# Gated delta stage: 16x16 substitution split in two, two panel splits moved, group loop written out

## The chip, the cores and the metric

The kernel runs on one core of one Trainium2 chip, in one launch. The metric is the device time in microseconds (us), the median of several executions. The profile is taken from one further execution.

## The reference, cut to what matters

The program computes a first transformer block and then a second one, for 512 tokens plus 16 meta tokens (528 in all), width 1024, in float32. The second block begins with a gated delta layer, and only that layer is touched here. Per head it solves, in each chunk of tokens, a unit lower triangular system and then runs a recurrence over the chunks:

```python
m = jnp.einsum('bhnid,bhnjd->bhnij', kb, k) * jnp.where(strict, decay, 0.0)
eye = jnp.eye(C, dtype=jnp.float32)
rhs = jnp.concatenate([vb, kb * jnp.exp(gc)[..., None]], axis=-1)
sol = lax.linalg.triangular_solve(m + eye, rhs, left_side=True, lower=True, unit_diagonal=True)
```

Before that, the projections of the normalised input pass through a causal convolution over four tokens and a SiLU, and the query and key heads are normalised to length 1.

## The kernel before, in words

**Tiling.** Features lie on the 128 partitions, tokens along the free axis. The 16 value heads are worked on in four groups (`NG` = 4, `gdn_group(g, first)`), four heads each. The chunks are one of 16 meta tokens (c = 0) and four of 128 tokens; `ORDER` is (1, 2, 3, 4, 0).

**Groups.** TensorE, VectorE, ScalarE and GpSimd run group 0 written out and groups 1 to 3 in a hardware loop (`mla_loop`, with `Fori`, so that waits are made on counts held in registers). The sync engine's queue is written out for all four groups already.

**Weights.** They come as a stream of panels of 512 KB through a ring of four slots (`raw`). For each panel the sync engine issues the load (`refill`, line 561), ScalarE makes the high part (`split_high`, line 291) and GpSimd the low part (`split_low`, line 296); `low(j)` in GpSimd's group is the split of the group's panel j + 2, since the splits run two panels ahead. `weights(j)` on the sync engine refills the slot of panel j, and waits until panel j has its low part, that is for `low(j - 2)`. Every product is three matmuls of high and low parts (`mm3`, lines 301 to 303).

**First part of a group.** TensorE makes eight projections `project(0..7)` into two pairs of PSUM banks in turn, 48 matmuls each. VectorE applies the convolution (`taps(t)`: line 1351 and three times line 1358), a clamp (line 510) between ScalarE's exponentials, and the product `gated(t)` (line 1368). A projection waits until the convolution has read its banks: `project(7)` waits for `taps(5)`, `project(8)` for `taps(6)`. `l2_scale` (line 1374) normalises query and key heads. Two more projections, `project(8)` and `project(9)`, belong to the output gate.

**The triangular system.** `first_m(c)` (line 1395) makes the matrix of a chunk on VectorE. The sync engine writes each of the four big chunks' matrices to DRAM (`m_out`, line 575) and reads their 16x16 diagonal blocks back, one block per partition (line 585, into `lane_w`). The queue's order is

```python
for j in range(7):
    weights(j)
m_out(1)
m_out(2)
weights(7)
m_out(3)
m_out(4)
```

and then the wait for all four, the read at line 585, `weights(8)` and `weights(9)`. On VectorE `substitute()` waits for the read (`LANES_IN`), sets the diagonal (line 1432), and inverts all blocks at once by forward substitution: for each k from 1 to 14 a product (line 1438) and a subtraction (line 1442), and at the end a transposed copy (line 1444). The sync engine, which waits for that copy, writes both results to DRAM (lines 590, 591) and reads them back by rows (line 594, into `row_w` and `row_wt`).

GpSimd then masks them into the matrices `TN` (line 644, four times), VectorE into `U` (`turned_16`, line 1450, four times). From there 15 steps (`STEPS`) join blocks of 16 to blocks of 128: in each, GpSimd masks a matrix (line 655, buffer `CL`), TensorE multiplies twice (lines 2161 and 2126) and transposes, ScalarE and VectorE copy and subtract. Steps 4, 9 and 14 are those of the short chunk of 16 tokens. The first step needs the first mask of line 655. After the steps comes the recurrence over the chunks, with parts of the gate's projections and of the output projection of the group before put between.

**Order around the change.** GpSimd issues `low(0)` to `low(7)`, the mask of the short chunk (line 637, needs `first_m(0)`), `low(8)`, `low(9)`, then waits for the rows. VectorE issues `gated(6)`, `substitute()`, `taps(7)`, `first_m(0)`, `attend(0)` (line 1409), `gated(7)`. TensorE waits for `attend(0)` (`g_at`) and for ScalarE's decays (`g_eabs`) ahead of `project(9)`.

Of the kernel before, what the change touches and what calls it, by code (L numbers as in the profile page):

```python
# [21 lines left out]
NG = 4  # L22
HG = 4
QUERY_TILES = (0, 2, 1, 3)
CHUNKS = 5
# [10 lines left out]
P_GDN = P_FF + 64  # L36
# [17 lines left out]
BLK = 16  # L54
# [33 lines left out]
def build(nc, A, out):  # L88
    ctx = ExitStack()
    with ctx:  # L90
# [173 lines left out]
        def sem(name):  # L264
            if name not in sems:
                sems[name] = ctx.enter_context(nc.semaphore(name))
            return sems[name]
# [220 lines left out]
        def gdn_panel(j, g):  # L488

            return (P_GDN + j, None, 0) if isinstance(g, int) and g == 0 else (P_GDN - 4 + j, g, 16)  # L490

# [9 lines left out]
        def mla_loop(engine, group):  # L501

            group(0, True)
            with engine.Fori(1, NG) as g:
                group(g, False)
# [26 lines left out]
        def gst(i, n, k):  # L532

            return i * n + k
# [5 lines left out]
        def _(sp):  # L540
# [26 lines left out]
            def gdn_group(g, first):  # L567
# [29 lines left out]
                for j in range(10, 12 if first else 16):  # L597
                    weights(j)
            for g in range(NG):
                gdn_group(g, g == 0)  # L600
            rest = STREAM - RING - (P_KV - RING)
# [12 lines left out]
        def _(pool):  # L614
# [13 lines left out]
            def gdn_group(g, first):  # L628
                def low(j):
                    p, i, length = gdn_panel(j, g)  # L630
                    split_low(pool, p + AHEAD, i, length)

                for j in range(8):
                    low(j)

                pool.wait_ge(sem("g_m1"), gst(g, CHUNKS, CHUNKS))
                pool.tensor_tensor(C0[0][0:META, :, 0:META], M[0][0:META, :, 0:META], level_mask(0, META),
                                   ALU.mult).then_inc(sem("g_c0"), 1)
                low(8)
                low(9)  # L640
                pool.wait_ge(sem("lanes_moved"), gst(g, ROWS_IN, ROWS_IN))
                pool.wait_ge(sem("l2_done"), gst(g, 4, 4))
                for c in ORDER[:LATER]:
                    pool.tensor_tensor(by_block(TN[c]), spread(row_w, c), block_mask(NEG_TRIL_16), ALU.mult)\  # L644
                        .then_inc(sem("g_t16"), 1)
                for s, (l, c) in enumerate(STEPS):
                    n = tokens(c)[1]
                    if s == 0 and not first:

                        pool.wait_ge(sem("z_lo"), gst(g, 4, 0))  # L650
                    if s == 1:
                        pool.wait_ge(sem("g_t16"), gst(g, LATER, LATER))
                    if s >= 2:
                        pool.wait_ge(sem("g_q"), gst(g, NS, s - 1))
                    pool.tensor_tensor(CL[s % 2][0:n, :, 0:n], M[c][0:n, :, 0:n], level_mask(l, n),  # L655
                                       ALU.mult).then_inc(sem("g_cl"), 1)
                for j in range(10, 12 if first else 16):
                    low(j)
            mla_loop(pool, gdn_group)
            for t in range(5):  # L660
# [16 lines left out]
        def _(act):  # L677
# [185 lines left out]
            def gdn_group(g, first):  # L863
# [161 lines left out]
                for t in range(4):  # L1025
                    high_y(t)
            mla_loop(act, gdn_group)
            def square_out(k):
# [122 lines left out]
        def _(dve):  # L1151
# [184 lines left out]
            def gdn_group(g, first):  # L1336
# [88 lines left out]

                def substitute():

                    w, wt = lane(lane_w), lane(lane_wt)
                    dve.wait_ge(sem("lanes_moved"), gst(g, ROWS_IN, LANES_IN))
                    if not first:  # L1430
                        dve.wait_ge(sem("z_lo"), gst(g, 4, 0))
                    dve.memset(lane_w[:, 0:BLK * BLK:BLK + 1], -1.0).then_inc(sem("g_lane"), 1)
                    for k in range(1, BLK - 1):
                        n = BLK - 1 - k
# [7 lines left out]
                        dve.tensor_tensor(below, below, tmp, ALU.subtract).then_inc(sem("g_lane"), 1)  # L1442
                    dve.wait_ge(sem("g_lane"), gst(g, LANE_OPS, LANE_OPS - 1))
                    dve.tensor_copy(wt, w.rearrange("p i j -> p j i")).then_inc(sem("g_lane"), 1)

# [30 lines left out]
                conv_clamp(4)  # L1476
                gated(4)
                taps(5)
                conv_clamp(5)
                l2_scale(2)  # L1480
                l2_scale(3)
                gated(5)
                taps(6)
                conv_clamp(6)
                gated(6)
                substitute()
                taps(7)
# [144 lines left out]
                low_y(3)  # L1632
            mla_loop(dve, gdn_group)
            for m in range(8):
# [174 lines left out]
        def _(pe):  # L1809
# [177 lines left out]
            def gdn_group(g, first):  # L1987
# [105 lines left out]
                project(8, 0)  # L2093
                pe.wait_ge(sem("g_at"), gst(g, CHUNKS, 1))
                pe.wait_ge(sem("g_eabs"), gst(g, CHUNKS * HG, CHUNKS * HG))
                pe.wait_ge(sem("l2_ln"), gst(g, 4, 4))
# [47 lines left out]
                for s, (l, c) in enumerate(STEPS):  # L2144
# [20 lines left out]
                    if s:  # L2165
                        join(s - 1)
                    if s == 1:
                        level_0()
                    if s - 2 in TURNED:
# [119 lines left out]
                out_tile(7)  # L2289
            mla_loop(pe, gdn_group)  # L2290
            pe.wait_ge(sem("g_vb"), CHUNKS * NG)
# [308 lines left out]
```

## Time and profile before

| | |
|---|---|
| median of 3 runs | 2154.03 us (2152.55 to 2160.12) |
| the profiled execution | 2150.23 us |
| its span, first to last instruction | 2148.4 us |
| mean granted TensorE clock | 0.951 of full speed |
| VectorE's substitution in the second group | 1044.68 to 1053.8 us |
| the same in the first group | 867.78 to 876.9 us |

PE is TensorE, DVE VectorE, ACT ScalarE, POOL GpSimd, SP the sync engine (SPq: its queue of DMA issues). Times in a timeline are microseconds from the start of the span; a row gives the start, the duration, engine, line, operation, output and inputs, and in brackets the idle time of the engine before it with what ended it. A row with x2, x3 and so on merges several instructions. The gated delta stage goes from about 808 to 1565 us, and its four groups begin near 808, 985, 1179 and 1374 us.

### The profile page before, as it was taken

How to read it: one execution, taken by the hardware profiler on the slowest of the kernel's cores; microseconds unless marked ns; L12 is line 12 of the kernel's file. 1: busy time of each engine (PE TensorE's matmuls, PEld its weight loads, DVE VectorE, ACT ScalarE, POOL GpSimd, SP SyncE). 2: the span in 40 equal slices, each digit the busy share in tenths (PEclk: the TensorE clock that was granted, in tenths of full speed). 3: DMA queues.
4: the chain of work that ended last, by engine and by line, in shares of the span. 5: the costliest groups of instructions: out<-in, count | busy, mean ns of one | idle time of the engine just before them, and what ended most of it. 6: DMA issues, size and time to landing. Idle time of an engine off the chain costs nothing.

```text
span 2148.4 us, 30354 instructions
## 1 busy us (share of the span) xinstructions
PE 1951.1 (91%) x11197; PEld 1620.1 (75%) x11269; DVE 1018.5 (47%) x1765; ACT 821.6 (38%) x1477; POOL 684.8 (32%) x334
## 2 busy tenths in 40 slices
PE   6999999799999979699699969988978999999994
PEld 4677777578778759688699969978967776777773
DVE  6422232613132255656746655575555455454544
ACT  4555632432232335226324523451335333333322
POOL 3132244343443422411431242125134212222212
PEclk9999999999999989889889989998989999999997
DMA  5112123132322303201301221131031111211111
GB/s 178 50 61 67 59 88 98 41 107 80 106 92 80 104 29 102 70 21 31 101 21 41 80 52 40 42 92 40 30 100 55 62 31 52 61 55 47 60 49 39
DMA packets 72898, 140.23 MB, mean 65 GB/s; under 512 B 30544, under 2 KB 40016, under 8 KB 72656
## 3 DMA queue, kind: packets, MB, share of 16 engines
q1 hardware_dynamic: 72064, 134.33, 20.2%
q10 hardware_dynamic: 720, 4.33, 0.5%
q8 instruction: 78, 1.28, 0.2%
q14 instruction: 36, 0.29, 0.0%
HBM read 129.13 MB, written 9.50 MB: 65 GB/s over the span
## 4 chain that ended last, share of the span: by engine, by line
PE 31%; issue 19%; POOL 8%; DVE 4%; ACT 2%; POOLq 0%; ACTq 0%; DVEq 0%
PE ps L301 6%; PE ps L302 6%; PE ps L303 6%; POOL wsp L296 5%; PE ps L2456 3%; PE ps L2425 2%; PE ps L2424 2%; POOL ov L644 1%; PE ps L2446 1%; PE ps L2161 1%; PE ps L2126 1%; POOL aux_f L655 1%; POOL work L655 1%; DVE aux_f L1358 1%; PE ps L2428 0%
## 5 line engine op out<-in xcount | busy, mean ns | idle before, releaser
L296 POOL TENSOR_TENSOR wsp<-raw,wsp 128x1024 fp32r<-128x1024 f32 x231 | 558.1, 2421 | 1282.1 <-ACT wsp L291 1282.1
L301 PE MATMUL ps<-h_split,wsp 128*128 128x264 f32 (+1 forms) x1488 | 524.5, 352 | 59.9 <-DVE ov L1409 41.0
L302 PE MATMUL ps<-h_split,wsp 128*128 128x264 f32 (+1 forms) x1488 | 511.5, 344 | 0.0
L303 PE MATMUL ps<-h_split,wsp 128*128 128x264 f32 (+1 forms) x1488 | 510.9, 343 | 0.0
L301 PEld LDWEIGHTS ps<-h_split,wsp 128*128 128x128 f32 x1488 | 289.3, 194 | 99.7 <-issue 56.2
L302 PEld LDWEIGHTS ps<-h_split,wsp 128*128 128x128 f32 x1488 | 288.9, 194 | 31.6
L303 PEld LDWEIGHTS ps<-h_split,wsp 128*128 128x128 f32 x1488 | 288.0, 194 | 32.4
L291 ACT ACTIVATE wsp<-raw 128x1024 fp32r<-128x1024 f32 x231 | 240.7, 1049 | 105.0 <-PE ps L303 103.7
L301 PE MATMUL ps<-y_split,wsp 128*128 128x512 f32 (+1 forms) x496 | 195.3, 394 | 12.9 <-DVE y_split L463 5.8
L302 PE MATMUL ps<-y_split,wsp 128*128 128x512 f32 (+1 forms) x496 | 191.7, 386 | 0.0
L303 PE MATMUL ps<-y_split,wsp 128*128 128x512 f32 (+1 forms) x496 | 191.0, 385 | 0.0
L301 PEld LDWEIGHTS ps<-y_split,wsp 128*128 128x128 f32 x496 | 94.8, 191 | 34.6 <-issue 14.6
L303 PEld LDWEIGHTS ps<-y_split,wsp 128*128 128x128 f32 x496 | 94.6, 191 | 19.2
L302 PEld LDWEIGHTS ps<-y_split,wsp 128*128 128x128 f32 x496 | 94.6, 191 | 18.6
L1293 DVE TENSOR_TENSOR work<-work,ps 128x512 f32<-128x512 f32 x32 | 22.0, 687 | 151.8 <-PE ps L303 151.8
L1761 DVE TENSOR_REDUCE tiny<-ps 128x1 f32<-128x144 f32 (+1 forms) x64 | 32.4, 506 | 112.6 <-PE ps L2428 112.6
L301 PE MATMUL ps<-y_late,wsp 128*128 128x264 f32 x256 | 75.8, 296 | 7.5 <-DVE work L1564 3.2
L1285 DVE TENSOR_TENSOR work<-work 128x512 f32<-128x512 f32 x32 | 29.4, 920 | 107.9 <-ACT work L819 107.9
L2456 PE MATMUL ps<-ov 128*128 128x128 f32 (+1 forms) x448 | 80.5, 307 | 0.0
L963 ACT ACTIVATE qs_f<-ps 128x512 f32<-128x512 f32 (+2 forms) x60 | 27.7, 462 | 133.3 <-PE ps L2161 133.3
L1358 DVE SCALAR_TENSOR_TENSOR aux_f<-ps,cwg,aux_f 128x528 f32<-128x528 f32 x96 | 73.8, 769 | 3.4
L2456 PEld LDWEIGHTS ps<-ov 128*128 128x128 f32 (+1 forms) x448 | 60.5, 192 | 18.5 <-issue 10.2
(346 smaller groups left out, 3237.1 us busy)
## 6 DMA issues: line engine op xcount, KB each, us to landing
raw<-in_w SPq DMA_DIRECT2D x231, 512.0 KB, 3.5
m_home<-ov SPq DMA_DIRECT2D x16, 256.0 KB, 4.4
x_home<-x_res ACTq DMA_DIRECT2D x1, 2112.0 KB, 6.7
x_res<-x_home ACTq DMA_DIRECT2D x4, 528.0 KB, 6.7
x_res<-in_x SPq DMA_DIRECT2D x4, 512.0 KB, 5.3
out<-x_res SPq DMA_DIRECT2D x8, 256.0 KB, 2.0
mats<-in_mats SPq DMA_DIRECT2D x1, 640.0 KB, 7.3
rope<-in_rope SPq DMA_DIRECT2D x1, 528.0 KB, 5.1
```

The source lines that it names most:

```text
L291: act.activation(wsp[:, s, 0, :], raw[:, s, :], ACT.Copy).then_inc(hi_ready, 1)
L296: pool.tensor_tensor(wsp[:, s, 1, :], raw[:, s, :], wsp[:, s, 0, :].bitcast(F32), ALU.subtract).then_inc(lo_ready, 1)
L301: pe.matmul(o, wh, xh, start=start, stop=False)
L302: pe.matmul(o, wh, xl, start=False, stop=False)
L303: return pe.matmul(o, wl, xh, start=False, stop=stop)
L655: pool.tensor_tensor(CL[s % 2][0:n, :, 0:n], M[c][0:n, :, 0:n], level_mask(l, n), ALU.mult).then_inc(sem("g_cl"), 1)
L1285: dve.tensor_tensor(relu2[b], relu[b], relu[b], ALU.mult).then_inc(sem("ff_sq"), 1)
L1358: dve.scalar_tensor_tensor(out=shifted, in0=x, scalar=cwg[:, 4 * t + k:4 * t + k + 1], in1=shifted, op0=ALU.mult, op1=ALU.add)\
L1761: dve.tensor_reduce(tiny[:, 4 + b:5 + b], s_ap, AX.X if i < 3 else AX.XY, ALU.max)\
L2424: pe.matmul(PS[:, bank_, 0:w], qn, KN[:, h, lo_:hi_], start=True, stop=False)
L2425: last = pe.matmul(PS[:, bank_, 0:w], qr, krope[r, lo_:hi_], start=False, stop=True)
L2456: last = pe.matmul(o_bank(b), VT[0:n, c, h * P:(h + 1) * P], PT[b][0:n, c, :], start=c == 0, stop=c == i + 1)
```

## The change: what it does

- VectorE: `substitute(k0, k1)` now does the rows k0 to k1 - 1. `substitute(1, 7)` stands between `gated(4)` and `taps(5)` and holds the wait for the blocks; `substitute(7, 15)` with the transposed copy stands between the clamp of tile 6 and `gated(6)`. `taps(6)` is moved ahead of `gated(5)`.
- GpSimd: `low(8)` and `low(9)` are taken from the place ahead of the row masks and put before the masks of steps 5 and 10 (`CHUNKS` is 5).
- TensorE: the waits for `attend(0)` and the decays are moved from ahead of `project(9)` to step 1 of the joining, ahead of `level_0()`.
- TensorE, VectorE, ScalarE and GpSimd: all four groups are written out (`gdn_groups`), with waits on constants.

```diff
--- before.py
+++ after.py
@@ -487,7 +487,12 @@
 
         def gdn_panel(j, g):
 
-            return (P_GDN + j, None, 0) if isinstance(g, int) and g == 0 else (P_GDN - 4 + j, g, 16)
+            return P_GDN + (16 * g - 4 if g else 0) + j, None, 0
+
+        def gdn_groups(group):
+
+            for g in range(NG):
+                group(g, g == 0)
 
         def mla_panel(j, g):
 
@@ -596,8 +601,7 @@
                       .then_inc(sem("lanes_moved"), 16)
                 for j in range(10, 12 if first else 16):
                     weights(j)
-            for g in range(NG):
-                gdn_group(g, g == 0)
+            gdn_groups(gdn_group)
             rest = STREAM - RING - (P_KV - RING)
             with sp.Fori(0, rest // RING) as i:
                 for s in range(RING):
@@ -636,8 +640,6 @@
                 pool.wait_ge(sem("g_m1"), gst(g, CHUNKS, CHUNKS))
                 pool.tensor_tensor(C0[0][0:META, :, 0:META], M[0][0:META, :, 0:META], level_mask(0, META),
                                    ALU.mult).then_inc(sem("g_c0"), 1)
-                low(8)
-                low(9)
                 pool.wait_ge(sem("lanes_moved"), gst(g, ROWS_IN, ROWS_IN))
                 pool.wait_ge(sem("l2_done"), gst(g, 4, 4))
                 for c in ORDER[:LATER]:
@@ -650,13 +652,15 @@
                         pool.wait_ge(sem("z_lo"), gst(g, 4, 0))
                     if s == 1:
                         pool.wait_ge(sem("g_t16"), gst(g, LATER, LATER))
+                    if s in (CHUNKS, 2 * CHUNKS):
+                        low(7 + s // CHUNKS)
                     if s >= 2:
                         pool.wait_ge(sem("g_q"), gst(g, NS, s - 1))
                     pool.tensor_tensor(CL[s % 2][0:n, :, 0:n], M[c][0:n, :, 0:n], level_mask(l, n),
                                        ALU.mult).then_inc(sem("g_cl"), 1)
                 for j in range(10, 12 if first else 16):
                     low(j)
-            mla_loop(pool, gdn_group)
+            gdn_groups(gdn_group)
             for t in range(5):
                 split_low(pool, P_KV - 4 + AHEAD + t)
             norm_add_odd(pool, "nC", NK, ALL)
@@ -1024,7 +1028,7 @@
                     act.wait_ge(used, turn(p + 1, i, length))
                 for t in range(4):
                     high_y(t)
-            mla_loop(act, gdn_group)
+            gdn_groups(gdn_group)
             def square_out(k):
                 norm_square(act, "nC", lambda m: accT[:, m, :], NK, k, lambda m: (sem("g_add"), 8 * NG + m + 1))
             split_high(act, P_KV - 2)
@@ -1423,14 +1427,15 @@
                     dve.tensor_tensor(TN[0][0:n, :, 0:n], mat_h(IDENT, n), C0[0][0:n, :, 0:n], ALU.subtract)\
                        .then_inc(sem("g_t0"), 1)
 
-                def substitute():
+                def substitute(k0, k1):
 
                     w, wt = lane(lane_w), lane(lane_wt)
-                    dve.wait_ge(sem("lanes_moved"), gst(g, ROWS_IN, LANES_IN))
-                    if not first:
-                        dve.wait_ge(sem("z_lo"), gst(g, 4, 0))
-                    dve.memset(lane_w[:, 0:BLK * BLK:BLK + 1], -1.0).then_inc(sem("g_lane"), 1)
-                    for k in range(1, BLK - 1):
+                    if k0 == 1:
+                        dve.wait_ge(sem("lanes_moved"), gst(g, ROWS_IN, LANES_IN))
+                        if not first:
+                            dve.wait_ge(sem("z_lo"), gst(g, 4, 0))
+                        dve.memset(lane_w[:, 0:BLK * BLK:BLK + 1], -1.0).then_inc(sem("g_lane"), 1)
+                    for k in range(k0, k1):
                         n = BLK - 1 - k
                         tmp = lane_tmp[:, 0:n * k].rearrange("p (i j) -> p i j", j=k)
                         below = w[:, k + 1:BLK, 0:k]
@@ -1440,8 +1445,9 @@
                            .then_inc(sem("g_lane"), 1)
                         dve.wait_ge(sem("g_lane"), gst(g, LANE_OPS, 2 * k))
                         dve.tensor_tensor(below, below, tmp, ALU.subtract).then_inc(sem("g_lane"), 1)
-                    dve.wait_ge(sem("g_lane"), gst(g, LANE_OPS, LANE_OPS - 1))
-                    dve.tensor_copy(wt, w.rearrange("p i j -> p j i")).then_inc(sem("g_lane"), 1)
+                    if k1 == BLK - 1:
+                        dve.wait_ge(sem("g_lane"), gst(g, LANE_OPS, LANE_OPS - 1))
+                        dve.tensor_copy(wt, w.rearrange("p i j -> p j i")).then_inc(sem("g_lane"), 1)
 
                 def turned_16(c):
 
@@ -1475,15 +1481,16 @@
                 taps(4)
                 conv_clamp(4)
                 gated(4)
+                substitute(1, 7)
                 taps(5)
                 conv_clamp(5)
                 l2_scale(2)
                 l2_scale(3)
+                taps(6)
                 gated(5)
-                taps(6)
                 conv_clamp(6)
+                substitute(7, BLK - 1)
                 gated(6)
-                substitute()
                 taps(7)
                 conv_clamp(7)
                 first_m(0)
@@ -1630,7 +1637,7 @@
                 low_y(1)
                 low_y(2)
                 low_y(3)
-            mla_loop(dve, gdn_group)
+            gdn_groups(gdn_group)
             for m in range(8):
                 if m % 2 == 0:
                     dve.wait_ge(used, P_KV - 4 + m // 2 + 1)
@@ -2091,8 +2098,6 @@
                 project(7, 2, 4)
                 pe.wait_ge(sem("g_conv"), gst(g, 8, 7))
                 project(8, 0)
-                pe.wait_ge(sem("g_at"), gst(g, CHUNKS, 1))
-                pe.wait_ge(sem("g_eabs"), gst(g, CHUNKS * HG, CHUNKS * HG))
                 pe.wait_ge(sem("l2_ln"), gst(g, 4, 4))
                 project(9, 6)
                 last_of = {}
@@ -2165,6 +2170,8 @@
                     if s:
                         join(s - 1)
                     if s == 1:
+                        pe.wait_ge(sem("g_at"), gst(g, CHUNKS, 1))
+                        pe.wait_ge(sem("g_eabs"), gst(g, CHUNKS * HG, CHUNKS * HG))
                         level_0()
                     if s - 2 in TURNED:
                         turn_u(s - 2)
@@ -2287,7 +2294,7 @@
                 out_tile(6, 2)
                 norm_o(CHUNKS - 1)
                 out_tile(7)
-            mla_loop(pe, gdn_group)
+            gdn_groups(gdn_group)
             pe.wait_ge(sem("g_vb"), CHUNKS * NG)
             pe.wait_ge(sem("g_oln"), CHUNKS * NG)
             for t in range(4):
```

## Rows read from the trace of the kernel before

**Rows 1.** The page: busy time of the engines (share of the span), instructions.

```profile
PE 1951.1 (91%) x11197; PEld 1620.1 (75%) x11269; DVE 1018.5 (47%) x1765; ACT 821.6 (38%) x1477; POOL 684.8 (32%) x334
```

**Rows 2.** TensorE's waits, second group (985 to 1175 us).

```profile
PE ps L301 <- DVE ov L1409: 10.3, 1, 10.3
PE ps L2161 <- POOL work L655: 5.9, 1, 5.9
```

**Rows 3.** Timeline of the sync engine's queue, second group: start, us, line, transfer.

```profile
1034.10 0.35 SPq L561 DMA_DIRECT2D raw<-in_w  x1
1034.54 0.94 SPq L575 DMA_DIRECT2D m_home<-ov  x2
1039.43 0.36 SPq L585 DMA_DIRECT2D ov<-m_home  x1
1041.06 6.75 SPq L561 DMA_DIRECT2D raw<-in_w  x2
1053.85 0.33 SPq L590 DMA_DIRECT2D w_home<-ov  x1
...
1056.46 0.94 SPq L594 DMA_DIRECT2D work<-w_home  x1
```

**Rows 4.** Time from issue to landing of line 585, over the four groups.

```profile
DMA to landing us min/median/max: 2.9/3.0/3.0
```

**Rows 5.** Time from issue to landing of line 594, over the four groups.

```profile
DMA to landing us min/median/max: 2.9/3.3/3.8
```

**Rows 6.** Timeline of VectorE, second group: start, us, line, operation, [idle before].

```profile
1031.31 0.76 DVE L1351 TENSOR_SCALAR aux_f<-ps,cwg 128x528 f32<-128x528 f32 x1
...
1036.46 0.71 DVE L1374 SCALAR_TENSOR_TENSOR work<-work,ov 128x528 f32<-128x528 f32 x1 [0.22 <-ACT ov L894]
...
1038.30 0.76 DVE L1351 TENSOR_SCALAR aux_f<-ps,cwg 128x528 f32<-128x528 f32 x1
...
1044.68 0.07 DVE L1432 MEMSET ov<- 128x16 f32 x1
...
1045.21 2.26 DVE L1438 TENSOR_TENSOR work<-ov 128x26 f32<-128x26 f32 x1
...
1049.66 0.22 DVE L1438 TENSOR_TENSOR work<-ov 128x56 f32<-128x56 f32 x1
...
1060.82 8.71 DVE L1450 TENSOR_TENSOR aux_f<-work,mats 128x512 f32<-128x512 f32 x4
```

**Rows 7.** Timeline of GpSimd, second group.

```profile
1031.68 2.39 POOL L296 TENSOR_TENSOR wsp<-raw,wsp 128x1024 fp32r<-128x1024 f32 x1 [7.08 <-ACT wsp L291]
1038.67 2.36 POOL L296 TENSOR_TENSOR wsp<-raw,wsp 128x1024 fp32r<-128x1024 f32 x1 [4.60 <-ACT wsp L291]
1045.00 2.43 POOL L296 TENSOR_TENSOR wsp<-raw,wsp 128x1024 fp32r<-128x1024 f32 x1 [3.97 <-ACT wsp L291]
...
1060.43 5.17 POOL L296 TENSOR_TENSOR wsp<-raw,wsp 128x1024 fp32r<-128x1024 f32 x2 [1.43 <-ACT wsp L291]
1065.56 6.29 POOL L644 TENSOR_TENSOR ov<-aux_f,mats 128x512 f32<-128x512 f32 x4
1071.81 1.25 POOL L655 TENSOR_TENSOR work<-ov,mats 128x512 f32<-128x512 f32 x1
...
1083.37 1.28 POOL L655 TENSOR_TENSOR aux_f<-ov,mats 128x512 f32<-128x512 f32 x1 [3.70 <-PE ps L2161]
```

**Rows 8.** Line 644 over all four groups: ns min/median/max.

```profile
L644 POOL TENSOR_TENSOR ov<-aux_f,mats x16: 1248/1702/1749, 888.7 to 1459.6; 128x512 f32<-128x512 f32 x16
```

**Rows 9.** TensorE by stretch: us, busy (instructions), granted clock, DMA.

```profile
1040.00:1048.97 8.97, 8.96 (x75) 1.00 0.40 90
...
1059.26:1063.26 4.00, 4.00 (x18) 0.50 0.06 9
```

**Rows 10.** TensorE's waits where the third group begins (1176 to 1183 us).

```profile
PE ps L301 <- issue: 2.7, 2, 1.7
```

**Rows 11.** TensorE's waits where the fourth group begins (1370 to 1378 us).

```profile
PE ps L301 <- issue: 2.1, 2, 1.4
```

## The prediction

> **What bounds the kernel now.** I read the page first: TensorE is busy 91% of the span [rows 1], so what a change in this stage is worth lies in TensorE's few waits. The view of its waits for the second group shows two that matter: 10.3 us ahead of `project(9)`, put down to line 1409 (`attend(0)`), and 5.9 us ahead of the first joining step, put down to GpSimd's first mask [rows 2]. The first comes from VectorE's order: `attend(0)` is issued behind the whole substitution and `taps(7)`. The second is the end of a chain: copy of the substitution done at 1053.8, write to DRAM issued 1053.85, last read back issued 1056.46 [rows 3], landed within 2.9 to 3.8 us [rows 5], so by 1060.3. Four masks of line 644 start at 1065.56, behind two panel splits that began at 1060.43, and the first step mask starts at 1071.81 [rows 7] and ends at 1073.06. From there the group runs its joining and recurrence, which the change leaves in order. So the question is not whether the 10.3 us go, but when that first step mask ends. All four groups have this shape; I work in the times of the second and multiply by four.
>
> **The change, part by part.**
>
> *Waits moved on TensorE.* `project(9)` no longer waits. Nothing of the 10.3 us is gained by that alone: `project(9)` took some 7.8 us from 1059.26 and ended near 1067, and TensorE then stood 5.9 us. The joining starts with the mask, not with TensorE.
>
> *First half of the substitution.* It needs the blocks on VectorE. The timeline of the queue says when they come: `weights(7)` goes out at 1034.10, the last two `m_out` at 1034.54, the read of the blocks at 1039.43 [rows 3], landing 2.9 to 3.0 us later [rows 4], at 1042.4. `weights(7)` waits for `low(5)`, which ends at 1031.68 + 2.39 = 1034.07 [rows 7]; that split follows ScalarE's work for tile 4, all ahead of the new wait, and the change touches neither it nor the queue's order. VectorE reaches `substitute(1, 7)` after `gated(4)`, at 1031.3, where `taps(5)` starts now [rows 6]. It will stand there for 1042.4 - 1031.3 = 11.1 us. Queued behind it are `taps(5)` and all the rest of VectorE's work; ScalarE's exponentials of tile 5, split 6, and TensorE's `project(7)` wait for that.
>
> Its own work: from the memset at 1044.68 to the product of k = 7 at 1049.66 is 4.98 us, in which one product took 2.26 us where a wider one takes 0.22 [rows 6]. That one ended at 1047.47, as GpSimd's split at 1045.00 + 2.43 did [rows 7]: the operation stood behind the split. Without that it is 4.98 - 2.1 = 2.9 us. GpSimd has nothing to do at 1042.4 to 1045.3, since `low(6)` waits for tile 5. End: 1045.3.
>
> *Tile 5, then tile 6.* From `taps(5)` at 1031.31 to the end of `l2_scale(3)` at 37.17 are 5.8 us [rows 6]: `taps(6)`, now next, starts at 1051.1 and ends 3.2 us later (one operation of 0.76 us [rows 6] and three like it), at 1054.3. Before it started at 1038.30. The move of `taps(6)` ahead of `gated(5)` saves the 1.2 us between these two rows, already counted so. `low(6)` came 7.36 us after the start of `taps(5)` [rows 6, 7]: now 1052.7 to 1055.05. `gated(5)`, two inputs in SBUF, stands behind it until 1055.05 and ends at 1055.6; the clamp ends at 1056.0.
>
> *Second half.* From 1049.66 to 1053.74, where `taps(7)` follows now, is 4.1 us of work [rows 6]. ScalarE's two exponentials and its split put `low(7)` 2.4 us after the clamp, as now (42.6 to 1045.00, [rows 7]): 1058.4 to 1060.8. The substitution stands behind it for 2.4 us again. End: 1056.0 + 4.1 + 2.4 = 1062.5, against 1053.8: 8.7 us late.
>
> The Trainium skill (SBUF — State Buffer, "Who interferes with whom") states that VectorE with two SBUF inputs and a GpSimd operation that reads SBUF exclude each other for the whole instruction. By that rule the two stops count in full, as above, and it speaks against placing the halves between the splits; a view of SBUF that gave both engines room would make the end 1059.5. The product of 2.26 us agrees with the rule.
>
> *Rows back.* From copy end to rows landed are now 1060.3 - 1053.8 = 6.5 us at most, 5.6 at least (landing 2.9). In the new order `weights(9)` is issued at 1060.8, 1.7 us ahead of the writes; in the queue now it is issued at 1047.5, the second of the pair at 1041.06 + 6.75 [rows 3], far ahead. A panel is 512 KB, a write 128 KB. I add 0.5 us: nothing at the low end; 1.6 us at the high end, about half of a panel's landing of the kind that delays the second pair of `m_out` (4.9 us from 1034.54 to 1039.43 against 3.0 for a read alone). Rows landed: 1062.5 + 6.5 + 0.5 = 1069.5.
>
> *Masks.* The two splits are gone from ahead of them, and the rows themselves set the start. Four masks of line 644 cost 1.25 us each alone and 1.70 each beside VectorE's `turned_16` [rows 8]; the four took 6.29 us because only the first ones met it [rows 7]. Now `turned_16` starts at the same time, so three meet it, and the first step mask too: 1.25 + 3 x 1.70 + 1.25 + 0.45 = 8.05 us. First step mask ends at 1077.55, against 1073.06: **4.5 us later in each group, 18 us in four**. Ends: with rows at 1068.1 and masks alone (6.25 us) 1074.4, +1.3; with rows at 1071.1 and a full 8.5 us 1079.6, +6.5.
>
> *Is TensorE later still?* `project(7)` starts when `taps(5)` is done, 1048.5, so TensorE stands some 13 us before it. After such a stand the granted clock is 0.50 for 4 us, 18 matmuls, against 75 in 8.97 us at full clock [rows 9]. First half to 1053.3, small products 1.3, second half 2.9: 1057.7. `taps(7)`, after `gated(6)`, starts at 1063.2 and is not held up. `project(8)` and `project(9)`, 5.8 each: 1069.4. TensorE has 8 us in hand, so this cold start costs nothing; if that cover went, it would cost some 2 us.
>
> *`low(8)` and `low(9)`.* 2.4 us each. At step 5 GpSimd stood 3.70 us before its mask [rows 7]: covered. Step 10 comes behind a short-chunk mask in the same way, with a stand that is some 0.5 us too short for the split; TensorE takes up a mask later than it is made. I cost both at nothing; without any cover they would cost 2.4 us each. Panels 10 and 11, and the later refills behind them (`weights(10)` and on), are wanted only in the recurrence.
>
> *Groups written out.* The passes of the loop that begin the third and fourth group show TensorE standing for 2.7 and 2.1 us with no releaser [rows 10, 11]. The first group, written out already, and the step from it to the second show no such stand. Gain 4.8 us; bounds 0 (if VectorE's copy of the group's scalars takes the place, as it held TensorE 0.8 us in the second group) and 6. The skill (Runtime: NRT & Kernel Launch, "Instruction fetch mechanics") says a taken branch outside the fetched window forces a fetch. The stands at the loop's turn agree.
>
> **Sum.** +18.0 - 4.8 = +13.2 us on the profiled execution's 2150.2 (2148.4 in the span, 1.8 around it): 2163.4. That execution lies 3.8 us under the median of 2154.0; put on the median the forecast is **2167 us**, +0.6%. Bounds of this case alone: 4 x 1.3 - 6 = -1 us, and 4 x 6.5 = +26; I hold +5 to +20 likely, 2159 to 2174.
>
> **Rivals.**
>
> *The wait is there, and the rest absorbs it: no change.* If GpSimd's splits fall between VectorE's operations and the writes don't queue, the copy ends at 1059.5, rows land at 1065.5, masks end at 1072.5 to 1074: about +0.4 per group, +1.6 - 4.8 = -3 us, 2151. Against it: the stop of 2.26 us, and the splits' places follow from the same exponentials.
>
> *The blocks are in time: faster.* If the read's landing did not stop VectorE at 1031.3, the first half would end at 1036.3 (one stop behind `low(5)`), all later steps 9.0 us earlier than in my account, and the first mask near 1068.5, as TensorE's `project(9)` ends by 59: -4.5 per group, -18 - 4.8 = -23 us, 2131. This decides as soon as the blocks land by about 1036.5; a landing at 1039.3 is break-even with the loop's gain. Only the queue's 1039.43 speaks against it, but plainly.
>
> *The late splits or long code cost.* A step mask behind `low(9)`, or fetching of straight code, at 1 to 2 us per group more: 2172. The first group's even run speaks against the code.
>
> **Chances.** Forecast case 0.66; absorbed 0.19; blocks in time 0.08; the last 0.07. A measurement of this kernel tells about 0.5%, 10.8 us, from no change. The forecast case lies above that in three of four of its outcomes, the last rival too: slower 0.55; same 0.34, from the lower part of the forecast case and the absorbed one; faster 0.11. Range 2150 to 2174: it leaves out the fast rival and the upper tail.
>
> **What the new profile would show.** Right: VectorE idle about 11 us before line 1432, released by the DMA of the blocks; TensorE idle about 13 us before `project(7)`, released by line 1358, none before `project(9)`, and about 8 us before the first line 2161; first step mask some 4.5 us later against the start of the group; no `issue` stands where groups begin. Wrong: a read of the blocks issued much before the time that answers to 1039.4, no stand at line 1432, or line 644 starting where it did.

## The result: 0.9% slower

| | before | changed |
|---|---|---|
| median | 2153.61 us (4 runs) | 2174.78 us (2173.19 to 2176.77, 4 runs) |
| profiled execution | 2150.23 us | 2175.55 us |
| span | 2148.4 us | 2173.8 us |
| mean granted clock | 0.951 | 0.943 |

The ratio is 1.0086 with a 95% interval of 1.0070 to 1.0101. The changed kernel is slower by 15 to 22 us by that interval. Forecast were 13 us more and a range up to 2174.

The page of the changed kernel, busy times and the costliest chain by engine:

```profile
PE 1955.4 (90%) x11197; PEld 1621.3 (75%) x11269; DVE 1016.7 (47%) x1765; ACT 821.7 (38%) x1477; POOL 685.0 (32%) x334
...
PE 44%; DVE 9%; ACT 3%; DMA 3%; issue 2%; POOL 2%; SPq 0%; ACTq 0%; POOLq 0%; DVEq 0%
```

TensorE has the same 11197 matmuls as before [rows 1] and is busy 4 us longer with them, at a lower mean clock; the other 21 of the 25 us by which the span grew are idle time. Its waits in the second group, which answer to [rows 2] (the window is shifted, since the group begins later):

```profile
PE ps L301 <- DVE aux_f L1362: 12.9, 1, 12.9
PE ps L2166 <- POOL work L659: 9.1, 1, 9.1
PE ps L2024 <- DVE cwg L1347: 2.8, 1, 2.8
```

The wait for `attend(0)` is gone. In its place stands one for line 1362, the last operation of `taps(5)`, ahead of `project(7)`, and the wait for the first step mask has grown from 5.9 to 9.1 us. VectorE's timeline says why (answers to [rows 6]; line 1437 is the memset, 1443 and 1447 the product and subtraction, 1355 begins a tile's convolution, 1372 is `gated`, 1450 the transposed copy):

```profile
1056.91 0.07 DVE L1437 MEMSET ov<- 128x16 f32 x1 [11.37 <-DMA ov<-m_home]
...
1059.69 0.76 DVE L1355 TENSOR_SCALAR aux_f<-ps,cwg 128x528 f32<-128x528 f32 x1
...
1065.47 0.76 DVE L1355 TENSOR_SCALAR aux_f<-ps,cwg 128x528 f32<-128x528 f32 x1
...
1068.56 1.42 DVE L1372 TENSOR_TENSOR work<-aux_f 128x528 f32<-128x528 f32 x1
...
1070.24 0.20 DVE L1443 TENSOR_TENSOR work<-ov 128x56 f32<-128x56 f32 x1
...
1072.93 2.28 DVE L1447 TENSOR_TENSOR ov<-ov,work 128x36 f32<-128x36 f32 x1
...
1076.11 0.39 DVE L1450 COPY aux_f<-ov 128x256 f32<-128x256 f32 x1
```

VectorE stands 11.37 us, released by the DMA of the blocks. In the second half one subtraction takes 2.28 us, and `gated(5)` 1.42 where it takes 0.71 otherwise. GpSimd's timeline (answers to [rows 7]) and the sync engine's (answers to [rows 3]):

```profile
1067.04 2.37 POOL L296 TENSOR_TENSOR wsp<-raw,wsp 128x1024 fp32r<-128x1024 f32 x1 [18.82 <-ACT wsp L291]
1072.70 2.46 POOL L296 TENSOR_TENSOR wsp<-raw,wsp 128x1024 fp32r<-128x1024 f32 x1 [3.29 <-ACT wsp L291]
...
1084.72 6.75 POOL L646 TENSOR_TENSOR ov<-aux_f,mats 128x512 f32<-128x512 f32 x4 [2.42 <-DMA work<-w_home]
1091.44 1.25 POOL L659 TENSOR_TENSOR work<-ov,mats 128x512 f32<-128x512 f32 x1
1092.66 1.26 POOL L659 TENSOR_TENSOR aux_f<-ov,mats 128x512 f32<-128x512 f32 x1
...
1099.35 2.35 POOL L296 TENSOR_TENSOR wsp<-raw,wsp 128x1024 fp32r<-128x1024 f32 x1
...
1111.33 2.36 POOL L296 TENSOR_TENSOR wsp<-raw,wsp 128x1024 fp32r<-128x1024 f32 x1
```

```profile
1048.25 0.35 SPq L566 DMA_DIRECT2D raw<-in_w  x1
1048.69 0.94 SPq L580 DMA_DIRECT2D m_home<-ov  x2
1053.92 0.36 SPq L590 DMA_DIRECT2D ov<-m_home  x1
1069.44 6.10 SPq L566 DMA_DIRECT2D raw<-in_w  x2
1076.53 0.33 SPq L595 DMA_DIRECT2D w_home<-ov  x1
...
1081.07 0.94 SPq L599 DMA_DIRECT2D work<-w_home  x1
```

The queue is as before: the read of the blocks goes out only after `weights(7)` and the two writes behind it. The two long operations of VectorE fall into the splits of GpSimd at 1067.04 and 1072.70. The splits at 1099.35 and 1111.33 are the late `low(8)` and `low(9)`; TensorE shows no wait for a later step mask than the first (line 659 stands once in the rows above).

**Where the time went.** I cut the gated delta stage of both traces at the same events. Each number is a sum over the four groups, changed less before:

| stretch | us |
|---|---|
| read of the blocks issued, to first step mask done | +19.0 (4.6, 5.1, 4.3, 5.0) |
| first step mask done, to last step mask begun | +2.5 (109.9 to 112.4) |
| from there to the next group's read of the blocks (three edges) | -1.7 (+2.9, -2.7, -1.9) |
| ends of the stage | 0.0 |
| stage: first convolution to first addition of the output | 779.15 against 759.38, +19.8 |
| ahead of the stage (unchanged code) | 821.05 against 814.92, +6.1 |
| behind the stage (unchanged code) | 573.6 against 574.1, -0.5 |

The 6.1 us ahead of the stage are not the change's. TensorE is busy all the time there, and the windows from 85 to 330 us (us, busy and instructions, granted clock) show a lower mean clock in that one execution. An experiment below, whose code there is the same, does not show it. First the changed kernel, then the experiment e11:

```profile
85.00:330.00 245.00, 243.85 (x1042) 0.97 0.19 63
```

```profile
85.00:330.00 245.00, 243.85 (x1068) 1.00 0.20 67
```

In the changed kernel's profile the clock fell to its lower level for some 3 us near 90, 137, 187 and 232 us. Of the thirteen profiles of this study the same windows show 0.97 in three, 0.99 in three and 1.00 in seven, whatever the kernel. The medians differ by 21.2 us, the ratio makes it 18.5; both are near the stage's 19.8.

### The profile page after: what moved, and what is told of

Its sections match the earlier page's. It is cut to its first block, busy times and chain, and to the rows that moved or that the text cites. A ratio compares the mean times of both kernels' runs of the same rounds, so it can differ in the third digit from the quotient of the medians.

```text
span 2173.8 us, 29564 instructions
## 1 busy us (share of the span) xinstructions
PE 1955.4 (90%) x11197; PEld 1621.3 (75%) x11269; DVE 1016.7 (47%) x1765; ACT 821.7 (38%) x1477; POOL 685.0 (32%) x334
## 4 chain that ended last, share of the span: by engine, by line
PE 44%; DVE 9%; ACT 3%; DMA 3%; issue 2%; POOL 2%; SPq 0%; ACTq 0%; POOLq 0%; DVEq 0%
PE ps L301 8%; PE ps L302 7%; PE ps L303 7%; PE ps L2463 3%; PE ps L2432 2%; PE ps L2166 2%; PE ps L2131 2%; PE ps L2431 2%; DVE aux_f L1362 2%; PE ps L2024 1%; POOL ov L646 1%; PE ps L2453 1%; DMA m_home<-ov 1%; PE ps L2147 1%; DVE ov L1399 1%
## 5 line engine op out<-in xcount | busy, mean ns | idle before, releaser
L301 PE MATMUL ps<-y_split,wsp 128*128 128x512 f32 (+1 forms) x496 | 195.5, 394 | 12.9 <-DVE y_split L463 5.8
L879 ACT ACTIVATE aux_f<-aux_f 128x528 f32<-128x528 f32 x32 | 20.5, 642 | 141.2 <-DVE aux_f L1362 141.2
L2463 PEld LDWEIGHTS ps<-ov 128*128 128x128 f32 (+1 forms) x448 | 59.9, 190 | 18.3 <-issue 9.7
```

Source lines behind the costliest of these rows:

```text
L301: pe.matmul(o, wh, xh, start=start, stop=False)
L2463: last = pe.matmul(o_bank(b), VT[0:n, c, h * P:(h + 1) * P], PT[b][0:n, c, :], start=c == 0, stop=c == i + 1)
```

## The experiments

All ratios are to the kernel before, measured on the same chip. Line numbers in rows are those of the kernel in question; the operations tell which is which.

The experiments were not all measured on the same chip, and the stretch ahead of the stage, whose code is the same in all of them, took between 812.9 and 821.1 us in the profiles. Two experiments are therefore best compared by the stage alone, in the profile of each (first convolution to first addition of the output, as in the table above):

| kernel | stage, us |
|---|---|
| before | 759.4 |
| changed | 779.2 |
| e1, written out | 756.3 |
| e2, one piece | 738.3 |
| e3, early blocks | 746.0 |
| e4, lows back | 793.0 |
| e5, ahead of gated(6) | 728.9 |
| e6, ahead of taps(6) | 755.8 |
| e7, waits back | 773.2 |
| e8, waits moved alone | 756.9 |
| e10, e6 with the refill behind | 732.5 |
| e11, changed with the refill behind | 773.3 |
| e12, first mask early | 725.1 |

### e1_written_out: only the groups written out

```diff
-            mla_loop(pool, gdn_group)
+            gdn_groups(gdn_group)
...
-            mla_loop(pe, gdn_group)
+            gdn_groups(gdn_group)
```

> The kernel before with only the four groups written out. Theory of the prediction: the stands at the loop's turns go (2.7 and 2.1 us), so -4.8 us, 2149 us, ratio 0.998, and the blocks' first read is issued where it was (863 us). Rival (writing out costs in the stages ahead: in the changed kernel's trace that first read came 6 us later, with short drops of the granted clock near 100 to 240 us that the trace of before lacks): +1 to +3 us, first read near 869 us.

Measured: 2146.98 us (12 runs), ratio 0.9962 (0.9951 to 0.9973): -8.2 us. The first read of the blocks was issued at 862.8, where it was 863.04 before. The rival falls. In the stage the gain is 3.1 us (756.3): the stands at the two loop turns are gone, but at the edge from the first to the second group TensorE now waits 2.8 us for VectorE's copy of the convolution weights, where it waited 0.8 in the same view of before. The waits in e1's second group:

```profile
PE ps L301 <- DVE ov L1414: 10.0, 1, 10.0
PE ps L2166 <- POOL work L660: 5.3, 1, 5.3
PE ps L2022 <- DVE cwg L1348: 2.8, 1, 2.8
```

That copy of 32 columns takes 2.35 us in the changed kernel, beside GpSimd's split (1001.57 and 1001.43 us), and 0.17 in the kernel before. What the median gains beyond the stage is not located: the stretch behind the stage was 571.0 us in this one profile, and varies from 571.0 to 574.7 over the profiles.

### e2_one_piece: the change without the split of the substitution

```diff
-                substitute(1, 7)
...
-                substitute(7, BLK - 1)
                 gated(6)
+                substitute(1, BLK - 1)
```

> The changed kernel with the substitution in one piece behind gated(6), as before; late low parts, moved waits, taps(6) ahead of gated(5) and written-out groups stay. Theory (the wait of the first half for the blocks is the loss): no idle time of VectorE ahead of the memset; rows land as before, masks start with them at some 1060.3 in the old times, first step mask ends 4.7 us earlier than before in each group: 4 x -4.7 - 4.8 = -24 us, 2130 us, ratio 0.989. Rival (late low parts, moved waits or long code are part of the loss): 2137 us or more.

Measured: 2129.82 us, ratio 0.9878 (0.9861 to 0.9895): 26 us faster than before and 45 us faster than the changed kernel. The split alone costs that; by the stage it is 40.8 us. The late low parts, the moved waits and the written-out groups are no loss; the rival falls.

### e3_early_blocks: the change, with the blocks read ahead of weights(7)

```diff
                 m_out(2)
-                weights(7)
                 m_out(3)
                 m_out(4)
                 sp.wait_ge(sem("lanes_moved"), gst(g, ROWS_IN, M_OUT))
                 sp.dma_start(lane(lane_w), ...)
+                weights(7)
```

> The changed kernel with the sync queue's order altered: the writes of chunks 3 and 4 and the read of the blocks ahead of the refill weights(7). Theory: the read is issued near 1031.1 in the old times instead of 1039.4, lands at 34, VectorE stands 2.7 us instead of 11.4; everything behind comes 8.3 us earlier, first step mask ends 3.7 us earlier than before: 4 x -3.7 - 4.8 = -20 us, 2134 us, ratio 0.991. Rival (the order of the queue is not what makes the blocks late, or refill and writes only change places): 2165 to 2175 us.

Measured: 2139.92 us, ratio 0.9934 (0.9916 to 0.9952): 35 us faster than the changed kernel (33.2 in the stage), and faster than before, with the split kept. VectorE's stand for the blocks fell to 4.27 us in the second group; TensorE's before `project(7)` to 5.8. The order of the queue is what made the blocks late. It is 6 us short of my number. The blocks landed some 1.5 us later than I had put it, behind the longer row of writes, and the result's write still follows a refill, as in the changed kernel:

```profile
1024.70 2.87 SPq L580 DMA_DIRECT2D m_home<-ov  x4
1031.41 0.36 SPq L589 DMA_DIRECT2D ov<-m_home  x1
...
1054.93 0.33 SPq L595 DMA_DIRECT2D w_home<-ov  x1
...
1059.53 0.94 SPq L599 DMA_DIRECT2D work<-w_home  x1
```

From 1054.93 to the last read's issue are 4.6 us, against 2.6 in [rows 3]. In the other three groups it is 3.2 to 3.5 us.

### e4_lows_back: the change, with low(8) and low(9) where they were

```diff
                 pool.tensor_tensor(C0[0]...).then_inc(sem("g_c0"), 1)
+                low(8)
+                low(9)
...
-                    if s in (CHUNKS, 2 * CHUNKS):
-                        low(7 + s // CHUNKS)
```

> The changed kernel with low(8) and low(9) back ahead of the row masks. Theory: ScalarE's split for low(8) comes behind tile 7's exponentials, so the two splits of GpSimd end some 3.9 us after the rows have landed and hold the masks up by that: +16 us on the changed kernel, 2190 us, ratio to before 1.017. Rival (the splits put between the joining steps cost there what they save): 2175 to 2180 us.

Measured: 2183.92 us, ratio 1.0137 (1.0120 to 1.0154): by the medians 9 us slower than the changed kernel, between the two theories. The traces side with the theory: from the blocks' read to the first step mask the four groups take 16.9 us more than in the changed kernel, where I had put 16, and the stage 13.9 us more. In these two profiles the stretch ahead of the stage, which is not the edit's, was 8.1 us shorter in e4, so the whole times show less of it. So the late low parts are a gain of the change, not a loss, of some 3.5 us per group in the stage.

### e7_waits_back: the change, with TensorE's two waits where they were

```diff
+                pe.wait_ge(sem("g_at"), gst(g, CHUNKS, 1))
+                pe.wait_ge(sem("g_eabs"), gst(g, CHUNKS * HG, CHUNKS * HG))
                 pe.wait_ge(sem("l2_ln"), gst(g, 4, 4))
                 project(9, 6)
...
-                        pe.wait_ge(sem("g_at"), gst(g, CHUNKS, 1))
-                        pe.wait_ge(sem("g_eabs"), gst(g, CHUNKS * HG, CHUNKS * HG))
                         level_0()
```

> The changed kernel with TensorE's two waits back ahead of project(9). Theory (moving them is worth nothing, since joining waits for the step mask): attend(0) is done at 1082.2 in the changed kernel's times, project(9) takes 7.8 us cold and ends at 1090, the first step mask at 1092.7: no change, 2175 us, within 4 us. Rival (the removed wait was worth its 10 us, hidden under the new one): 2190 us or more.

Measured: 2168.01 us, ratio 1.0059 (1.0043 to 1.0076): 6.8 us faster than the changed kernel (5.9 in the stage). Both theories miss. In the second group the waits come and go as told: 3.6 us ahead of `project(9)` and 2.9 ahead of the joining, in place of 9.1:

```profile
PE ps L301 <- DVE aux_f L1362: 13.2, 1, 13.2
PE ps L301 <- DVE ov L1413: 3.6, 1, 3.6
PE ps L2168 <- POOL work L659: 2.9, 1, 2.9
```

The joining itself, from the first step mask done to the last one begun, took 106.4 us in the four groups against 112.4, and the clock is why. Here are the first 4 us of the joining and the 4 us behind them, in the first and second group, for the kernel before, for the changed kernel and then for e7:

```profile
896.15:900.15 4.00, 3.94 (x20) 0.55 0.00 0
900.15:904.15 4.00, 4.00 (x39) 1.00 0.00 0
1073.06:1077.06 4.00, 3.94 (x18) 0.50 0.00 0
1077.06:1081.06 4.00, 4.00 (x38) 0.98 0.00 0
```

```profile
906.75:910.75 4.00, 3.94 (x18) 0.50 0.00 0
910.75:914.75 4.00, 4.00 (x31) 0.76 0.00 0
1092.69:1096.69 4.00, 3.94 (x18) 0.50 0.00 0
1096.69:1100.69 4.00, 4.00 (x37) 0.96 0.00 0
```

```profile
904.60:908.60 4.00, 3.40 (x29) 1.00 0.00 0
908.60:912.60 4.00, 4.00 (x36) 1.00 0.01 4
1088.41:1092.41 4.00, 3.94 (x22) 0.61 0.00 0
1092.41:1096.41 4.00, 4.00 (x39) 1.00 0.00 0
```

After a stand of 8 to 9 us TensorE begins the joining at the lower of its two clock levels (granted 0.50) and keeps it for 4 to 6 us. With the idle time cut into two stands, of which the one just ahead of the joining is short (1.3 to 2.9 us in e7), the clock is up at once in the first and the fourth group and partly in the others. Against e7, having the idle time in one place ahead of the joining costs some 6 us.

The kernel before does not have this advantage either. It stands 5.8 to 6.2 us ahead of the joining, begins it at 0.50 to 0.55 in all four groups, and needs 109.9 us for it. Nor does a longer stand cost more by itself: e3, with 7.2 to 9.4 us, needs 109.9 us too, e2, with 12.7 to 13.5, 112.8, and e8, with 18.2 to 18.3, 110.8. What makes the low level last longer in some groups than in others is not shown.

### e8_waits_moved_alone: e1 with only the two waits moved

The same edit the other way round, on e1.

> The written-out kernel with, in addition, only TensorE's two waits moved to step 1. Theory: the 10 us ahead of project(9) go, and come back ahead of the first joining step, which keeps its time: 2147 us, ratio 0.996, as written out alone. Rival (the longest wait of TensorE is worth its time): 4 x -10 us at most, 2107 us, or a part of it.

Measured: 2148.24 us, ratio 0.9963 (0.9944 to 0.9983), against 2146.98 of e1. TensorE's longest wait was removed and gave nothing (the stage is 0.6 us longer). It came back whole, as the wait view of the second group says:

```profile
PE ps L2164 <- POOL work L660: 18.3, 1, 18.3
```

10.0 and 5.3 us in e1 are 18.3 us in one piece here. `project(9)` no longer runs cold: it took 8.8 us in e1, from 1061.02 to 1069.8, and takes some 5.8 here, which is the difference of 3.0. TensorE is done sooner and stands longer.

### e11_changed_refill_behind: the change, with weights(9) behind the result's transfers

```diff
                 weights(8)
-                weights(9)
                 sp.wait_ge(sem("g_lane"), gst(g, LANE_OPS, LANE_OPS))
...
-                for j in range(10, 12 if first else 16):
+                for j in range(9, 12 if first else 16):
                     weights(j)
```

> The changed kernel with weights(9) behind those writes and reads. Theory (refill 1.7 us ahead of the writes delays them: from the copy to the landed rows were 8.2 us, where the kernel before has 6.5): first step mask 1.7 us earlier in each group, -7 us, 2168 us, ratio to before 1.0055. Rival (the transfers don't disturb each other): 2175 us, 1.0086.

Measured: 2164.70 us (7 runs), ratio 1.0043 (1.0027 to 1.0058): 10 us faster than the changed kernel, of which 5.8 are in the stage. The direction is that of the theory, the size is not. The writes' landing fell from 2.4 and 2.6 us to 1.7 and 1.8 (medians of four). From the write's issue to the last read's issue it is 2.6 us in three groups, as before, where the changed kernel has 3.3 to 3.5; but in the second group it is 4.3 still, where the changed kernel has 4.5, so the delay there is not this refill's, and its cause is open. The first step mask came only 0.4 us earlier per group on average, and 2.6 us came from warmer clocks in the joining (109.8 us against 112.4).

### e5_ahead_of_gated6: early blocks, one piece ahead of gated(6)

```diff
-                substitute(1, 7)
...
                 conv_clamp(6)
-                substitute(7, BLK - 1)
+                substitute(1, BLK - 1)
                 gated(6)
```

together with e3's edit of the queue.

> The changed kernel with the queue's early read of the blocks and the substitution in one piece ahead of gated(6) instead of split. Theory (what counts is when the whole substitution ends, as long as VectorE never stands for the blocks): it starts right at the clamp of tile 6, 2.0 us earlier than in the one-piece kernel: 4 x -2.0 on 2130 us = 2122 us, ratio 0.985. Rival (TensorE or the splits of GpSimd are the limit by now): 2130 us, unchanged.

Measured: 2120.22 us, ratio 0.9837 (0.9820 to 0.9853). As expected: without the stand, time follows the end of the substitution. The stage is 9.5 us shorter than in e2, where I had put 8.

### e6_ahead_of_taps6, and e10: still earlier

```diff
                 l2_scale(3)
+                substitute(1, BLK - 1)
                 taps(6)
```

> The same, with the substitution in one piece still earlier, ahead of taps(6). Theory: the rows come some 5 us earlier than in the one-piece kernel, but taps(6) comes 9 to 11 us later, project(8) waits for it with a cold clock behind, and project(9) ends near 65.5 in the old times, later than the first step mask (63.6): joining starts 2.9 us earlier than in the one-piece kernel, 4 x -2.9 on 2130 us = 2118 us, ratio 0.983. Rival (work of TensorE held up costs in full, as in the changed kernel): 2140 us or more.

Measured: 2145.84 us, ratio 0.9958 (0.9940 to 0.9975). A miss by 28 us, and not by the rival's cause. VectorE's copy was done at 1048.4, and the write of its result was issued at 1058.20:

```profile
1036.22 21.54 SPq L566 DMA_DIRECT2D raw<-in_w  x3
1058.20 0.33 SPq L595 DMA_DIRECT2D w_home<-ov  x1
...
1063.86 0.95 SPq L599 DMA_DIRECT2D work<-w_home  x1
```

The first row merges three refills and ends at 1057.8 with the third, `weights(9)`. That one waits for `low(7)`, which ended at 1057.4; `low(7)` follows tile 6, and tile 6 now comes after the substitution. I had moved work on one queue past a wait that stands on another. e10 puts `weights(9)` behind, as e11 does:

> The kernel with the substitution ahead of taps(6), and in addition the refill weights(9) behind the writes and reads of the substitution's result in the sync engine's queue. In the trace of the former the copy was done at 1048.4 and its write was issued only at 1058.2, since the queue stood at weights(9) for the late low(7). Theory: the rows land near 1055, the first step mask ends near 1063, and the end of project(9), 1065.9, sets the joining, 9.6 us earlier than in that kernel: 4 x -9.6 on 2146 us = 2107 us, ratio 0.978, and somewhat less as TensorE stands only once. Rival (the late taps(6) was the loss): 2140 to 2146 us.

Measured: 2126.40 us, ratio 0.9858 (0.9838 to 0.9878): 19 us of the 38 expected. The first step mask was begun at 1063.75 and done at 1065.02, but now VectorE is late, and TensorE waits 3.2 us for a U mask. Its `gated(7)` (line 1371), and behind it the U masks (line 1455) that the joining needs, met GpSimd's six masks in a row:

```profile
1059.17 7.63 DVE L1371 TENSOR_TENSOR work<-aux_f 128x528 f32<-128x528 f32 x1 [0.52 <-ACT aux_f L522]
...
1067.48 2.48 DVE L1455 TENSOR_TENSOR aux_f<-work,mats 128x512 f32<-128x512 f32 x4
```

```profile
1058.70 5.08 POOL L645 TENSOR_TENSOR ov<-aux_f,mats 128x512 f32<-128x512 f32 x4
1063.75 1.27 POOL L658 TENSOR_TENSOR work<-ov,mats 128x512 f32<-128x512 f32 x1
1064.98 1.25 POOL L658 TENSOR_TENSOR aux_f<-ov,mats 128x512 f32<-128x512 f32 x1
```

`gated(7)` takes 7.63 us where a `gated` takes 0.71 (median): it began within the first of GpSimd's masks and ended 0.6 us after the sixth.

### e12_first_mask_early: e5 with the first step mask taken forward

```diff
-                for j in range(8):
+                for j in range(6):
                     low(j)
+                pool.wait_ge(sem("g_m1"), gst(g, CHUNKS, 1))
+                if not first:
+                    pool.wait_ge(sem("z_lo"), gst(g, 4, 0))
+                step_mask(0)
+                low(6)
+                low(7)
...
-                for s, (l, c) in enumerate(STEPS):
...
+                for s in range(1, NS):
...
+                    step_mask(s)
```

`step_mask(s)` is the operation that makes the mask of step s.

> The kernel of e5_ahead_of_gated6 with the mask of the first joining step taken from behind GpSimd's four row masks to behind low(5), where GpSimd stands anyway; all work is kept. Theory (the joining is gated by the chain blocks, substitution, rows, masks, and the first step mask is its last link): step 0 starts some 3 us earlier, step 1 and all behind it by the 1.7 us of one mask; 4 x -1.7 on 2120 us = 2113 us, ratio to before 0.981. Rival (the row masks alone or a cold clock set the start): 2119 to 2121 us.

Measured: 2116.88 us (5 runs), ratio 0.9812 (0.9794 to 0.9829). Faster than e5, by the ratios 5 us of the 7 expected, with intervals that overlap a little, and by the stage 3.8. The mask of the second step, counted from the read of the blocks, is done 1.6 us earlier in three groups and 2.1 in one, for the 1.7 expected. It is the fastest version found, 1.9% faster than before and 2.7% faster than the changed kernel.

## Why the prediction was right

**The blocks are late and VectorE stands for them: shown.** Forecast 11.1 us of stand, measured 11.4. e3 cuts the stand to 4.3 us with the queue's order alone and gains 35 us; e2 takes it away by undoing the split and gains 45.

**The steps behind it: right to half a microsecond.** From the issue of the blocks' read to the copy's end I had 23.1 us; measured are 22.6, with the two stops of VectorE behind GpSimd's splits where they were put. TensorE's stand before `project(7)` was 12.9 us for 13, and no wait before `project(9)` was left.

**The transfers of the result: term too small.** I added 0.5 us for the refill ahead of them, 7.0 us in all from the copy's end to the masks' start. Measured are 7.0, 8.2, 7.2 and 7.9 in the four groups. The 6.5 us that I took for the kernel before was an upper bound worked out from the range of the landing times, and the experiment e11 leaned on it. My upper end for the rows, 1071.1, was a slip too: 1062.5 + 6.5 + 1.6 are 1070.6, which makes the upper bound of the sum 24 us and not 26.

**First step mask 4.5 us later per group: measured 4.7** (mean of four), 19.0 us in all for 18.0.

**"This cold start costs nothing", and the joining left at its old time: half right.** The sentence held for the first of TensorE's two stands, which has 8 us in hand. For the second stand my sum has no term at all. It grew from some 6 us to between 7.8 and 9.1, and the joining behind it took 2.5 us more in the four groups, at a low clock level that lasted longer. That the longer stand is the cause is not shown: the group with the longest stand lost least (0.1 us, against 0.6 to 1.0), and e3, with stands as long, shows no loss. What e7 shows is that the moved waits, which I took at nothing, cost some 6 us in this kernel against having them back.

**Groups written out, -4.8 us: term too large, the most of the miss.** The loop's stands are gone, and -4.6 us of the edges bear it out. But the first edge is 2.9 us longer: VectorE's small copy, which I had named as the lower bound, met a split, and TensorE waits 2.8 us for it in place of 0.8. That is 2.0 of the 2.9 us; the rest is not located. Net -1.7 us. Alone (e1) it gave 3.1 us in the stage.

So the sum was 18.0 - 4.8 = 13.2, and what the stage shows is 19.0 + 2.5 - 1.7 + 0.0 = 19.8 us. The mechanism was right. Three terms were too low or too hopeful, all to the same side: the masks by 1.0 us, the joining by 2.5 and the written-out groups by 3.1. The median, 2174.78, lies 0.8 us above my range; the ratio, put on the 2154.0 us that the range was built on, gives 2172.6, inside it. That a loss half as large again as forecast lies at the range's edge and not well beyond it is owed to the range's width. Of the rivals, the absorbing one is refuted by the stops in the trace, and the one with the blocks in time by the 11.37 us. What stays open: the part of e1's gain that lies outside the stage, how long the low clock level lasts in the joining, the second group's slower transfers, and why some executions show the short clock drops ahead of the stage.

## What to carry to other kernels

Before a consumer is moved ahead, look in the producer's queue for the time at which its data are issued, and at what stands ahead of them there: here 7 of the 11 us of stand per group hung on one refill between two writes (e3), and the reorder that pays was in the sync engine's queue, not on VectorE. The longest wait of the busiest engine can be worth nothing (e8); follow the chain that releases the next thing behind it. In e7 TensorE's idle time was worth 6 us more when the stand just ahead of the joining was under 3 us; where that stand is over 5 us anyway, as in e1, one long stand (e8) cost no more than two. So look at the last stand ahead of the work, not only at the sum.

## What the runs showed of the hardware that I had not expected

VectorE operations with two SBUF inputs can stand behind a whole row of GpSimd operations, not only behind one: 7.63 us for `gated(7)` in e10, against 0.71. In the changed kernel such operations alternate with GpSimd's where VectorE has several in a row (line 646 at 1.7 us in place of 1.25). The Trainium skill (SBUF — State Buffer, "Who interferes with whom") has the exclusion for the whole instruction, and these rows agree; that the waiting side can lose several turns no run but e10's shows.

The lower clock level after a stand lasted for 4 to 6 us of the changed kernel's joining: in the rows above 18 matmuls in the first 4 us at a granted 0.50, and 31 and 37 in the next 4 us at 0.76 and 0.96. It did not follow the stand's length: after 5.3 us (e1, second group) the two stretches show 0.50 and 0.79, after 18.3 us (e8, first group) 0.50 and 0.94.
